# Forget gate and cached keys inside the value projection, key rows inside the query projection

## What is computed

```python
hk = _rmsnorm(x, p['kv_norm_g']) * (1 + sc_kv) + sh_kv
kvp = hk @ p['kv_w']                       # keys 1024 | values 1024 | forget 16
k_new, v_new = ...                         # 16 heads of 64
logf_new = jax.nn.log_sigmoid(kvp[..., 2 * FOX_W:] + p['kv_b_f'])
k_all = jnp.concatenate([past_k, k_new], axis=1)     # the same for v and logf
f_k = jnp.cumsum(logf_all, axis=1)
f_q = f_k[:, q_off:]
...
q = (h @ p['fox_w_q'][j]).reshape(B, T, FOX_HEADS, FOX_HEAD_DIM)
s = einsum(q, k_all) * hd ** -0.5 + F_q - F_k        # causal, softmax, times v_all
y = o.reshape(B, T, FOX_W) @ p['fox_w_o'][j]
```

## Time and profile before

| | us |
|---|---|
| median of 3 runs | 1879.63 |
| lowest, highest | 1878.85, 1882.75 |
| the profiled execution, its own time | 1878.21 |
| its span in the profile, first to last instruction | 1876.5 |
| PE busy | 1647.8 (88%) |
| DVE busy | 1152.5 (61%) |
| ACT busy | 972.6 (52%) |
| mean granted clock of TensorE, share of full | 0.934 |
| DMA moved | 421.23 MB, mean 224 GB/s |

### The profile page before, as it was taken

One profiled execution on the slowest core, in us unless ns is written; L12 is line 12 of the kernel. 1 busy time (PEld: TensorE's weight loads), 2 busy tenths in 40 slices (PEclk: granted clock), 3 DMA queues, 4 the chain that ended last, 5 costly groups with the idle time before them and its releaser, 6 DMA issues. The chain is left out here.

```text
span 1876.5 us, 26584 instructions
## 1 busy us (share of the span) xinstructions
PE 1647.8 (88%) x10764; PEld 1404.6 (75%) x10764; DVE 1152.5 (61%) x1222; ACT 972.6 (52%) x1147; POOL 45.0 (2%) x148
## 2 busy tenths in 40 slices
PE   4699689956999995886776799999999999999995
PEld 2699366645999994885565688888888888888884
DVE  1684251144444334241843688979898888889895
ACT  1443422246433335240544577767776777677774
POOL 2121010000000000000000000000000000000000
PEclk9899799978999997897987899999999999999998
DMA  8630859663554443223020399999999999999991
GB/s 257 205 112 26 302 182 364 232 190 90 135 145 142 140 136 117 83 95 123 1 91 1 123 369 364 356 314 356 365 353 336 334 357 363 344 327 351 375 355 69
DMA packets 260574, 421.23 MB, mean 224 GB/s; under 512 B 12167, under 2 KB 125008, under 8 KB 260432
## 3 DMA queue, kind: packets, MB, share of 16 engines
q1 hardware_dynamic: 253824, 413.45, 64.4%
q10 hardware_dynamic: 6620, 6.00, 1.0%
HBM read 414.34 MB, written 5.07 MB: 224 GB/s over the span
## 5 line engine op out<-in xcount | busy, mean ns | idle before, releaser
L2496 DVE TENSOR_TENSOR w_lo_late<-raw,w_hi_late 128x2048 fp32r<-128x2048 f32 x264 | 600.8, 2289 | 93.6 <-ACT w_hi_late L2428 92.0
L2428 ACT ACTIVATE w_hi_late<-raw 128x2048 fp32r<-128x2048 f32 x264 | 505.3, 1918 | 172.9 <-PE bank L352 172.8
L350 PE MATMUL bank<-w_hi_late,hg_hi 128*128 128x512 f32 (+1 forms) x768 | 290.2, 378 | 1.1 <-DVE w_lo_late L2496 0.5
L352 PE MATMUL bank<-w_hi_late,hg_lo 128*128 128x512 f32 (+1 forms) x768 | 286.0, 372 | 0.0
L351 PE MATMUL bank<-w_lo_late,hg_hi 128*128 128x512 f32 (+1 forms) x768 | 285.5, 372 | 0.0
L271 DVE TENSOR_TENSOR w_lo_main<-raw,w_hi_main 128x2048 fp32r<-128x2048 f32 (+1 forms) x50 | 112.3, 2250 | 142.4 <-ACT w_hi_main L264 142.4
L350 PEld LDWEIGHTS bank<-w_hi_late,hg_hi 128*128 128x128 f32 x768 | 144.7, 188 | 31.6 <-DVE w_lo_late L2496 7.4
L352 PEld LDWEIGHTS bank<-w_hi_late,hg_lo 128*128 128x128 f32 x768 | 144.7, 188 | 25.8
L351 PEld LDWEIGHTS bank<-w_lo_late,hg_hi 128*128 128x128 f32 x768 | 144.9, 189 | 24.1
L350 PE MATMUL bank<-w_hi_late,act_hi 128*128 128x512 f32 x352 | 138.3, 393 | 0.0
L352 PE MATMUL bank<-w_hi_late,act_lo 128*128 128x512 f32 x352 | 137.2, 390 | 0.0
(11 more groups left out here) (463 smaller groups left out, 2891.8 us busy)
## 6 DMA issues: line engine op xcount, KB each, us to landing
raw<-in_moe_w_gate SPq DMA_DIRECT2D x88, 1024.0 KB, 7.0
raw<-in_moe_w_up SPq DMA_DIRECT2D x88, 1024.0 KB, 7.3
raw<-in_moe_w_down SPq DMA_DIRECT2D x88, 1024.0 KB, 7.2
ada_delta<-in_ada_w SPq DMA_DIRECT2D x40, 1024.0 KB, 8.6
raw<-in_gdn_w_in SPq DMA_DIRECT2D x16, 1024.0 KB, 6.5
raw<-in_ffn_w_gate SPq DMA_DIRECT2D x22, 512.0 KB, 4.0
raw<-in_ffn_w_up SPq DMA_DIRECT2D x22, 512.0 KB, 5.3
ada_start<-in_ada_w SPq DMA_DIRECT2D x8, 1024.0 KB, 14.3
```

What stands on the lines that cost most here:

```text
L350: pe.matmul(out, w_hi, x_hi, start=start, stop=False)
L352: return pe.matmul(out, w_lo, x_hi, start=False, stop=stop)
L2428: act.activation(k.w_hi[:, m % SPL, :], k.raw[:, m % RAW, :], ACT.Copy).then_inc(k.hi_ready, 1)
L2496: dve.tensor_tensor(k.w_lo[:, m % SPL, :], k.raw[:, m % RAW, :], k.w_hi[:, m % SPL, :], ALU.subtract).then_inc(k.raw_split, 1)
```

## The change

`forget_phase` and `key_phase` go, and so do the small blocks ahead of them. Their work is placed as follows.

- `past_k` is loaded where `v_past` was, ahead of the key projection. `v_past` is loaded by SP at the start of `attention_phase`, and PE waits for it ahead of its first product with it.
- `value_phase` takes in the forget gate and the cached keys. In slab 0 a logit product follows each of the 24 steps (a step is three products). In slab 1 PE turns groups 0 to 3 of the cached keys, one after each sixth step; in slab 2 the running sums follow each third step in eight parts; in slab 3 the turns 4 to 7. ACT's and DVE's parts are placed between their splits. Banks 6 and 7 serve all of this.
- `copy_phase` and `dense_tiles` can be given rows to turn: in the query projection two groups of new keys are turned after each of slabs 0 to 2, DVE copies them into the space of `past_k`, and SP stores key and value rows behind its loads. The wait for all stores moves into `attention_phase`.

The core of the diff:

```diff
@@ dense_tiles
         last.then_inc(k.split_read, 1)
+        if turn is not None and s < 3:
+            turn(2 * s)
+            turn(2 * s + 1)
@@ copy_phase
             for n in range(n0, n0 + n_slabs):
                 k.load(sp, n + RAW)
+            if rows is not None:
+                rows.sp(sp)
...
-            k.ahead_lo(dve, n0 + n_slabs - 1 + AHEAD)
+            for s in range(n_slabs):
+                k.ahead_lo(dve, n0 + s + AHEAD)
+                if rows is not None and s < 3:
+                    rows.dve(dve, 2 * s)
+                    rows.dve(dve, 2 * s + 1)
@@ value_phase, sync
             for n in range(n0, n0 + n_slabs):
                 k.load(sp, n + RAW)
+            sp.wait_ge(ready, 1)
+            k.store(sp, 0, k.o["logf"][0][0]..., logf[:, 0:2, :])
+            k.store(sp, 0, k.o["logf"][1][0], logf[0:TS, 2, :])
@@ value_phase, tensor
+            def sums(n):
+                if n == 0:
+                    pe.wait_ge(ready, 1)
+                    pe.wait_ge(copied, 4)
+                if n < 2:
+                    rows(own_sums[:, n * P:(n + 1) * P], prompt_wide, n)
+                elif n < 6:
+                    rows(past_sums[:, (n - 2) * P:(n - 1) * P], sample_wide, n - 2)
+                elif n == 6:
+                    rows(own_sums[:, TP:T], sample_wide, 4)
+                else:
+                    columns()
+
+            def turn(n):
+                if n == 0:
+                    pe.wait_ge(caches_in, 32)
+                elif n == 1:
+                    pe.wait_ge(pre, 1)
+                elif n == 4:
+                    pe.wait_ge(sums_kept, 1)
+                if n % 4 >= 2:
+                    pe.wait_ge(copied, n - 1)
+                t, half = divmod(n, 2)
+                for q in range(4):
+                    last = pe.transpose(turn_bank(n)[:, q * P:(q + 1) * P], past_k[:, t, ...], k.ident[:])
+                last.then_inc(turned, 1)
...
-                last.then_inc(k.split_read, 1)
+                        if t == 2 and kt == KT - 1:
+                            last.then_inc(k.split_read, 1)
+                        step = t * KT + kt
+                        if s == 0:
+                            last = pe.matmul(logits[0:nt, t, :], h32[:, kt, t0:t0 + nt], k.wlf[:, kt, :], start=(kt == 0),
+                                             stop=(kt == KT - 1))
+                            if t == 2 and kt == KT - 1:
+                                last.then_inc(lf_done, 1)
+                        elif s == 2 and step % 3 == 2:
+                            sums(step // 3)
+                        elif s % 2 and step % 6 == 5:
+                            turn(4 * (s // 2) + step // 6)
@@ value_phase, scalar
                 k.ahead_hi(act, n0 + s + AHEAD)
+                if s == 1:
+                    act.wait_ge(pre, 1)
+                    run(act.activation(lt[:], logf[:], ACT.Abs))
+                    run(act.activation(lt[:], lt[:], ACT.Exp, scale=-1.0))
+                    act.activation(lt[:], lt[:], ACT.Ln, bias=1.0).then_inc(ln_ready, 1)
@@ value_phase, vector: the order on DVE
+            run(dve.memset(logf[:], 0.0))
+            run(dve.memset(wide, 0.0))
+            dve.wait_ge(caches_in, 32)
+            ...
+            k.ahead_lo(dve, n0 + AHEAD)
+            dve.wait_ge(lf_done, 1)
+            ...
+            last.then_inc(pre, 1)
+            k.ahead_lo(dve, n0 + 1 + AHEAD)
+            dve.wait_ge(ln_ready, 1)
+            ...
+            last.then_inc(ready, 1)
+            for n in range(4):
+                copy(n)
+            k.ahead_lo(dve, n0 + 2 + AHEAD)
+            dve.wait_ge(sums_done, 1)
+            ...
+            last.then_inc(sums_kept, 1)
+            k.ahead_lo(dve, n0 + 3 + AHEAD)
+            for n in range(4, 8):
+                copy(n)
@@ class KeyRows (the rows given to copy_phase)
+    def pe(self, pe, n):
+        if n >= 2:
+            pe.wait_ge(self.copied, n - 1)
+        for q in range(4):
+            last = pe.transpose(self.k.ps[6 + n % 2][0:nt, ...], self.k_new[:, 4 * half + q, t0:t0 + nt], self.k.ident[:])
+        last.then_inc(self.turned, 1)
+    def sp(self, sp):
+        sp.wait_ge(self.copied, 6)
+        ...
+            k.store(sp, 0, o[name][0][0]..., prompt)
+            k.store(sp, 0, o[name][1][0]..., sample)
@@ attention_phase
+        @block.sync
+        def _(sp):
+            sp.dma_start(v_past[:], k.i["cache_v"][0]...).then_inc(caches_in, 16)
+            sp.wait_ge(k.stores[0], k.n_store[0])
...
+                if p == 0:
+                    pe.wait_ge(caches_in, 48)
```

More of the change, by code:

```diff
@@ L1616, in _, with copy_phase @@
             low(pieces - 1)
-def copy_phase(k, n0, n_slabs, n_k, x_hi, x_lo, dst, scale=1.0, renewal=None):
+def copy_phase(k, n0, n_slabs, n_k, x_hi, x_lo, dst, scale=1.0, renewal=None, rows=None):
     nc = k.nc
@@ L1729, in _, with value_phase @@
             low(n_slabs - 1)
-def value_phase(k, h_hi, h_lo, v_new):
+def value_phase(k, h_hi, h_lo, h32, v_new, logf, past_logf, f_cols, neg_rows, past_k, k_past_t, caches_in):
     nc, n0, n_slabs = k.nc, k.first["kv_w2"], 4
@@ L1741, in _, with rows @@
                 k.load(sp, n + RAW)
+            sp.wait_ge(ready, 1)
+            k.store(sp, 0, k.o["logf"][0][0].rearrange("(t p) h -> p t h", p=P), logf[:, 0:2, :])
+            k.store(sp, 0, k.o["logf"][1][0], logf[0:TS, 2, :])
         @block.tensor
         def _(pe):
+            def rows(out, tiles, j):
+                n = tiles[j][1]
+                for q in range(j + 1):
+                    src, nk = tiles[q]
+                    rhs = k.tri_incl[0:nk, 0:n] if q == j else k.ones[0:nk, 0:n]
+                    pe.matmul(out, src, rhs, start=(q == 0), stop=(q == j))
@@ new lines, in columns @@
+            def columns():
+                for t, (tiles, j) in enumerate(((prompt, 0), (prompt, 1), (sample, 4))):
+                    n = tiles[j][1]
+                    for q in range(j + 1):
+                        src, nk = tiles[q]
+                        lhs = k.tri_incl[0:nk, 0:n] if q == j else k.ones[0:nk, 0:n]
+                        pe.matmul(col_sums[0:n, t * FH:(t + 1) * FH], lhs, src, start=(q == 0), stop=(q == j))
+                for q in range(5):
+                    src, nk = sample[q]
+                    lhs = k.tri_incl[0:nk, 0:TS] if q == 4 else k.ones[0:nk, 0:TS]
+                    last = pe.matmul(col_sums[TS:P, 2 * FH:3 * FH], lhs, src, start=(q == 0), stop=(q == 4))
+                last.then_inc(sums_done, 1)
@@ new lines, in sums @@
+            def sums(n):
[21 more added lines that the diff above has]
+                for q in range(4):
+                    last = pe.transpose(turn_bank(n)[:, q * P:(q + 1) * P], past_k[:, t, (4 * half + q) * P:(4 * half + q + 1) * P],
+                                        k.ident[:])
+                last.then_inc(turned, 1)
@@ L1835, in _, with copy @@
+            run = k.dve_chain.on(dve)
+            def copy(n):
+                t, half = divmod(n, 2)
+                dve.wait_ge(turned, n + 1)
+                dve.tensor_copy(k_past_t[:, 4 * half:4 * half + 4, t * P:(t + 1) * P],
+                                turn_bank(n)[:].rearrange("p (q n) -> p q n", q=4)).then_inc(copied, 1)
             run(dve.memset(logf[:], 0.0))
-            run(dve.memset(wide[:], 0.0))
+            run(dve.memset(wide, 0.0))
+            dve.wait_ge(caches_in, 32)
@@ L1837, in _ @@
             for c in (0, TS):
                 dve.tensor_copy(wide[:, 0:4, c:c + FH], past_logf[:])
+            k.ahead_lo(dve, n0 + AHEAD)
             dve.wait_ge(lf_done, 1)
             for t, (t0, nt) in enumerate(TOKEN_TILES):
-                last = dve.tensor_tensor(logf[0:nt, t, :], ps[0:nt, t, :], k.b_forget[0:nt], ALU.add)
+                last = dve.tensor_tensor(logf[0:nt, t, :], logits[0:nt, t, :], k.b_forget[0:nt], ALU.add)
             last.then_inc(pre, 1)
+            k.ahead_lo(dve, n0 + 1 + AHEAD)
@@ L1856, in _ @@
-        @block.scalar
-        def _(act):
-            run = k.act_chain.on(act)
-            act.wait_ge(pre, 1)
-            run(act.activation(lt[:], logf[:], ACT.Abs))
-            run(act.activation(lt[:], lt[:], ACT.Exp, scale=-1.0))
-            act.activation(lt[:], lt[:], ACT.Ln, bias=1.0).then_inc(ln_ready, 1)
-        @block.sync
-        def _(sp):
-            sp.wait_ge(ready, 1)
-            k.store(sp, 0, k.o["logf"][0][0].rearrange("(t p) h -> p t h", p=P), logf[:, 0:2, :])
-            k.store(sp, 0, k.o["logf"][1][0], logf[0:TS, 2, :])
```

158 lines of the change are left out of this document (50 added, 108 removed).

## The result

The changed kernel takes 1863.26 us (median of 4 runs, 1860.38 to 1863.40), the kernel before beside it 1881.19 (4 runs, 1878.85 to 1883.80): a ratio of 0.9898, 95% interval [0.9883, 0.9913]. That is 17.9 us faster where 25.4 were forecast, and 1.3 us above the upper end of the range. The profiled execution took 1860.38 us, its span is 1858.7.

The account below looks back on a forecast made before the run. Stages were taken to follow strictly, with 120.0 us from key projection to attention's first score to shorten. Terms summed to -25.4 us: 1878.21 to 1852.8 on the profiled execution, plus 1.4 for the median, 1854.3; range 1849 to 1862.

Parts of the forecast that it names:

- (c): Rival: clock stays low through the whole value block, +38 us, result 1892; chance 0.03.
- Start of the value block: Ahead of the value projection: the forget stage vanishes and the first value product comes earlier, -21.28 us.
- Low clock at its start, the same 3.2 us as now: Value block, slab 0: 3.2 us of low clock as before; none would give -1.5 us, 6.8 would cost 1.5 more.
- Logits: Value block, slab 0: 24 added logit products cost 4.6 us plus 0.4 for low clock, +5.0.
- 32 turns of cached keys: Value block, slabs 1 and 3: 32 added turns at 0.129 us each, +4.1.
- exposed loads: Weight loads not hidden behind short products, some 16 inserted groups at 0.03 us each, +0.5, between 0 and 1.8.
- 24 turns of new keys: Query projection, after slabs 0 to 2: 24 added turns at 0.129 us each, +3.1, at most 5.2.
- Behind the query projection: From ACT's last copy to attention's first score: load, turns, copies and stores go, a seam stays, -23.8 us.
- Waits costed at nothing: Value block: PE's new waits for DVE are covered, slacks 1, 0.2 and 0.3 us; a failed cover costs 0.5 to 2.
- Rival (b): A new wait replaces the old: PE stands 1 to 2 us at two or three places, result 1858.5; chance 0.08.
- (a): Rival: clock stays low through slab 0 of the value block, 23.5 us against 14.9, +8.6, result 1863; chance 0.14.
- (d): Rival: nothing comes of it because the weights' loads set the end, result 1879.6; chance 0.02.

Follow-up runs that it names:

- e2_pad1: The changed kernel with one more one-element DVE fill in slab 0 of the value block; 1847.39 us, ratio 0.9815 to the kernel before.
- e5: Kernel before with the forget gate inside the value projection, without turns there; keys, their load and key phase as before; 1869.49 us, ratio 0.9926.
- e7: Kernel before with only the transfers moved: cached keys loaded ahead of the key projection, cached values at attention; 1872.36 us, ratio 0.9948.
- e3: Kernel before with 120 one-element DVE fills between DVE's splits in the value phase; 1893.80 us, ratio 1.0057.
- e4: Kernel before with 128 one-element DVE fills between DVE's splits in the value phase; 1880.86 us, ratio 0.9992.
- e10: e2_pad1 with a block of eight chained DVE fills between query projection and attention while PE stands; 1867.72 us, ratio 0.9933.
- e12: e9 with four one-element ACT copies added to the new block; 1862.97 us, ratio 0.9893 to the kernel before.
- e9: e2_pad1 with a separate block ahead of the value projection for DVE's fills and forget-value copies (fills leave value_phase); 1866.54 us, ratio 0.9919.
- e11: e9 with the 24 logit products all behind slab 0 instead of between its groups; 1858.66 us, ratio 0.9878 to the kernel before.

## Why the prediction was wrong

**The step that failed** is in the first paragraph: "the stages follow each other strictly, and a stage that ends earlier moves all that follows". It held for 970 us, up to PE's last expert product, and failed at the exit of the expert loop. From that product to the end it took 35.3 us instead of 20.3 (1823.4 to 1858.7, 1856.2 to 1876.5), since DVE's list had become seven instructions shorter and its two empty passes took 15.4 us instead of 1.2. Neither this nor any other +15 stood among the rivals; (c), the one slower case, hung on the clock. The sum between the profiles is: 3.4 upstream, 29.3 between the seams, 0.1 from there to PE's last expert product, less 15.0, in all 17.8 (1876.5 - 1858.7).

That the result came within 1.3 us of the range is luck: two errors of opposite sign. Without the late exit the kernel takes 1847.39 us (e2_pad1), below the range's lower end of 1849, because the terms between the seams and attention gave more than was forecast.

The Trainium skill, "Runtime: NRT & Kernel Launch", section "Instruction fetch mechanics", says that a taken branch to a target outside the loaded pages waits for a fetch. The runs agree: the three jumps of the two empty passes took 3.4 to 3.6 us each in the changed kernel, with fetches beside them, and 0.29 to 0.32 in the kernel before. It was there to be weighed and wasn't.

**The terms between the seams**, forecast and measured:

- *Start of the value block*, -21.3: measured -21.8. Right.
- *Low clock at its start, the same 3.2 us as now*: wrong, there was none. PE paused 1.1 us and the clock stayed at 1.00, where before slab 0 took 1.7 us more than a bare one (797.81 - 787.63 = 10.18 against 8.44). That saved 1.7.
- *Logits*, +5.0 and a part of 0.5: measured 6.4. The price of the row of 32 instructions (0.109) is that of products in a row; between dense products each costs about 0.27.
- *Running sums*, +6.6: 23.47 us for slabs 2 and 3 of e5 less two bare ones is 6.6. Right.
- *32 turns of cached keys*, +4.1, and exposed loads, 0.5: slabs 1 to 3 take 35.5 us from the first copy to the last (777.29 to 812.80) and 32.3 without the turns in e5, so 3.2, or 0.10 a turn. Too dear. A part of it is that the row's 0.129 was taken where the clock was 0.90 at first; e7's row at 1.00 has 3.66/32 = 0.114. The rest is not accounted for.
- *24 turns of new keys*, +3.1: the time from the last copy of the values to the last of the queries grew by 1.9 (37.5 to 39.4).
- *Behind the query projection*, -23.8: measured 25.68 - 1.48 = 24.2. Right.
- *Waits costed at nothing*, with slacks of 0.2 and 0.3: right, PE is busy all of 14.82, 10.19 and 13.20 us, and all 12.12 us from there to 812.80. Rival (b) is out.

Together -29.3 instead of -25.4, mostly the clock and the turns, the logits going the other way.

**Attention.** "Attention and experts as long as now": for attention that was true only of the execution read. Its 73.8 us were the exception for that kernel: 75.3 in e3 and 78.1 in e4, whose attention and key phase are untouched. By these single profiles, an estimate, the change also gains some 4 us there against the medians: 29.3 and 4.3 are 33.6, and e2_pad1 is 34.7 below the median of the 13 runs beside it. "1 us either way" for the clock at attention's start was too narrow; e10 shows 4.3, and e12 3.1 with no longer pause than the changed kernel's.

**Rivals (a) and (c)**, a clock that stays low, did not come in the changed kernel, but their mechanism is real: in e9, 1.8 us more of pause bring slab 0 to 26.1 us, near the 23.5 that (a) had. What was wrong is what they were hung on. The share of dense work in slab 0 is the same in e9 and in the changed kernel; with the pause of 2.9 us the clock was low in slab 0 of all three kernels that had it (e9, e11, e12), with that of 1.07 in none of the six. It also did not last through the block, as (c) had it: from slab 1 on, with few tiny products, the clock came back. (d) is out: all that PE gained reached the end of the expert stage.

**The rule on transposes.** With e7 there is a second case: behind a pause of 1.1 us PE did nothing but turns, at a granted clock of 1.00 in each window of 2 us from 862 to 870, 32 of cached keys in 3.7 us and 24 of new ones in 2.8 (5.4 before). The disagreement with the Trainium skill's "TensorE: Matmul & The Clock Gate", Part 4, stands.

What stays open: why the engine fetches at every jump once the passes touch one page more, since no run varied the number of pages by itself; and what decides, between one execution and the next, how far the clock falls at attention's start, with the pause of 6.97 us that did not harm and the one of 1.51 that did.

## What to carry to other kernels

When a kernel holds a long loop that engines leave separately, look at when each engine arrives at the block behind it, before and after every change, also one that is far upstream: if one arrives late with nothing to compute while code is fetched, add one harmless instruction to that engine ahead of the loop and measure again. Judge a change by its own stretch of the trace first, then account for the rest to the end; here a change worth 34 us showed 18. And closing a pause of PE can be worth more than the pause, when what follows is thin work that cannot bring the clock back; put the dense products first after a pause.

## What was not expected of the hardware

- A pair of a loop's own instructions on a boundary of code pages made two empty passes take 15.4 and 15.7 us on DVE instead of 1.2, and 13.7 to 15.1 on ACT instead of 1.0. It cost the kernel 15.3 to 15.5 us at the exit by DVE, and 6 to 7 by ACT.
- On DVE two places of the closing branch are costly, 1852 and 1979, and the neighbour one place further (1853) is free; the untouched kernel with 128 more instructions (1987) is as fast as with none (1859).
- A pause of 2.9 us of PE instead of 1.1 went with a granted clock of 0.50 instead of 1.00 for 26 us of uninterrupted work (e9, and 0.51 for 25.6 us in e12), where tiny fp32 products stood between the dense ones; with dense products alone the slab had a mean of 0.83 (e11).
- After a pause of 7.5 us attention's first 20 us ran at 0.67 in e4, after one of 1.5 us at 0.91 in e2, and the whole stage took 78.1 and 73.8 us; but the kernel before had 0.91 after 6.97 us, and e12 0.78 after 1.51.
